# A split-precision MLP up projection: from three matmuls of 256 columns a weight block to one of 512 and one of 256

## The reference

```
x = x + RMSNorm(mixer(RMSNorm(x)))
h = RMSNorm(x)                               # 256 x 2048
h = square(relu(h @ w_up[l])) @ w_down[l]    # w_up 2048 x 8192, w_down 8192 x 2048
x = x + RMSNorm(h)
```

## Time and profile before

| | us |
|---|---|
| median of 3 runs | 2249.34 |
| lowest, highest | 2249.28, 2250.1 |
| span of the profiled execution | 2248.1 |
| PE busy | 2216.5 (99% of the span) |
| DVE busy | 1319.9 (59%) |
| ACT busy | 1016.3 (45%) |

### The profile page before, as it was taken

The page is one execution under the profiler, slowest core; times in us unless marked ns, Lnnn a source line. Parts: engine busy times, 40 slices in busy tenths (PEclk is TensorE's granted clock), DMA queues, the critical chain, the costliest instruction groups (busy, mean ns, idle before and its releaser), DMA issues.

```text
span 2248.1 us, 39497 instructions
## 1 busy us (share of the span) xinstructions
PE 2216.5 (99%) x14282; PEld 2023.7 (90%) x14282; DVE 1319.9 (59%) x1528; ACT 1016.3 (45%) x1280; POOL 109.9 (5%) x112
## 2 busy tenths in 40 slices
PE   8999999999999999999999999999999999999997
PEld 8999888998998998898899988889989989988986
DVE  6777465655555455555578775657554545554555
ACT  5443464543444344344454435545434434443443
POOL 2141000000000000000001410000000000000000
PEclk9999999999999999999999999999999999999999
DMA  6555556556656656655645555655666566556565
GB/s 204 152 170 157 161 188 198 177 179 200 189 180 192 190 179 193 190 184 187 193 125 166 166 161 151 198 185 182 190 192 186 173 201 188 184 189 193 176 194 163
DMA packets 208448, 406.21 MB, mean 181 GB/s; under 512 B 12540, under 2 KB 12820, under 8 KB 207828
## 3 DMA queue, kind: packets, MB, share of 16 engines
q1 hardware_dynamic: 206660, 398.04, 57.3%
q10 hardware_dynamic: 992, 4.78, 0.6%
q0 software_dynamic: 688, 1.90, 0.4%
HBM read 402.58 MB, written 2.10 MB: 180 GB/s over the span
## 4 chain that ended last, share of the span: by engine, by line
issue 71%; PE 26%; DVE 1%; ACT 0%; POOL 0%; DMA 0%; DVEq 0%; POOLq 0%; ACTq 0%
PE acc L734 5%; PE acc L737 5%; PE acc L736 5%; PE acc L699 3%; PE acc L701 3%; PE acc L700 3%; PE M L838 1%; PE M L751 1%; DVE x_sb L1111 0%; PE M L859 0%; DVE xbcT L1177 0%; DMA wk<-in_ssd_out_norm 0%; PE M L879 0%; POOL st L393 0%; DVE w_lo L1028 0%
## 5 line engine op out<-in xcount | busy, mean ns | idle before, releaser
L1028 DVE TENSOR_TENSOR w_lo<-raw,w_hi 128x1024 fp32r<-128x1024 f32 x755 | 927.7, 1235 | 793.4 <-ACT w_hi L462 790.1
L462 ACT ACTIVATE w_hi<-raw 128x1024 fp32r<-128x1024 f32 x755 | 794.5, 1058 | 1026.8 <-PE acc L701 521.6
L734 PE MATMUL acc<-a_hi,w_hi 128*128 128x256 f32 x2912 | 828.4, 284 | 1.8 <-DVE w_lo L1028 1.8
L736 PE MATMUL acc<-a_lo,w_hi 128*128 128x256 f32 x2912 | 823.9, 283 | 0.0
L737 PE MATMUL acc<-a_hi,w_lo 128*128 128x256 f32 x2912 | 823.9, 283 | 0.0
L734 PEld LDWEIGHTS acc<-a_hi,w_hi 128*128 128x128 f32 x2912 | 558.6, 192 | 4.1 <-DVE w_lo L1028 2.7
L736 PEld LDWEIGHTS acc<-a_lo,w_hi 128*128 128x128 f32 x2912 | 558.7, 192 | 1.8 <-issue 1.0
L737 PEld LDWEIGHTS acc<-a_hi,w_lo 128*128 128x128 f32 x2912 | 558.7, 192 | 0.0
L699 PE MATMUL acc<-w_hi,u_hi 128*128 128x512 f32 x1280 | 498.6, 390 | 0.0
L700 PE MATMUL acc<-w_lo,u_hi 128*128 128x512 f32 x1280 | 498.0, 389 | 0.0
L701 PE MATMUL acc<-w_hi,u_lo 128*128 128x512 f32 x1280 | 498.0, 389 | 0.0
(11 more groups left out here) (218 smaller groups left out, 1049.2 us busy)
## 6 DMA issues: line engine op xcount, KB each, us to landing
raw<-in_w_up SPq DMA_DIRECT2D x256, 512.0 KB, 3.7
raw<-in_w_down SPq DMA_DIRECT2D x256, 512.0 KB, 4.5
raw<-in_w_in SPq DMA_DIRECT2D x179, 512.0 KB, 3.8
raw<-in_w_out SPq DMA_DIRECT2D x64, 512.0 KB, 4.6
zg<-in_post_mix_norm ACTq DMA_DIRECT2D x2, 1024.0 KB, 4.6
zg<-in_post_mlp_norm ACTq DMA_DIRECT2D x2, 1024.0 KB, 6.4
out<-x_sb SPq DMA_DIRECT2D x8, 256.0 KB, 2.8
x_sb<-in_x POOLq DMA_DIRECT2D x3, 512.0 KB, 7.3
```

The source lines that it names most:

```text
L462: act.activation(w_hi[:, c % RING], raw[:, c % RING], ACT.Copy).then_inc(sem["hi_ready"], 1)
L734: pe.matmul(o(m), w(w_hi, kk, m), a_hi[:, k], start=(k == 0 and m % 2 == 0), stop=False, skip_group_check=True)
L736: pe.matmul(o(m), w(w_hi, kk, m), a_lo[:, k], start=False, stop=False, skip_group_check=True)
L1028: dve.tensor_tensor(w_lo[:, c % RING], raw[:, c % RING], w_hi[:, c % RING].bitcast(F32), ALU.subtract).then_inc(sem["split_done"], 1)
```

## The change

The parts `a_hi` and `a_lo` become two halves of one tile, `a_both[:, k, 0]` and `a_both[:, k, 1]`. In an up block one matmul of 512 columns streams both through `w_hi`, and one of 256 columns streams `a_hi` through `w_lo`. hi·hi + lo·hi is summed in the left half of a bank and hi·lo in the right half, so a column tile `m` takes a whole bank and a block four. The eight banks are two groups, `wide[0]` (where `acc` lies) and `wide[1]` (where `M` lies), used by `j` = 0 and 1. The down blocks use `acc[1]` and `M[2], M[3]`. After an up block, ACT copies the right halves out, DVE adds the left halves to them, DVE forms relu(x)·x, ACT rounds it into `u_hi`, and DVE subtracts.

```
-        a_hi = sb("a_hi", [P, KT, SEQ], F32R)
-        a_lo = sb("a_lo", [P, KT, SEQ], F32R)
+        a_both = sb("a_both", [P, KT, 2, SEQ], F32R)
...
+        wide = [ctx.enter_context(nc.psum_tensor(f"wide{i}", [P, 4, CB], F32)) for i in range(2)]
+        acc = [[wide[0][:, 2 * i + j] for j in range(2)] for i in range(2)]
+        M = [wide[1][:, i] for i in range(4)]
+        down_acc = [acc[1], [M[2], M[3]]]
+        a_hi, a_lo = a_both[:, :, 0], a_both[:, :, 1]
...
+            def wide_chunk(c, j, lo_ready=None):
...
+                for kk in range(CK):
+                    k = c * CK + kk
+                    for m in range(CB // P):
+                        pe.matmul(wide[j][:, m], w(w_hi, kk, m), a_both[:, k].rearrange("p a s -> p (a s)"),
+                                  start=(k == 0), stop=False, skip_group_check=True)
+                        ins = pe.matmul(wide[j][:, m, 0:SEQ], w(w_lo, kk, m), a_hi[:, k], start=False,
+                                        stop=(k == KT - 1), skip_group_check=True)
+                ins.then_inc(sem["mm_done"], 1)
...
# PE, up_pair
-                        pe.wait_ge(*left(l, B_MLP + j, 0, q * QB + i))
+                        if first:
+                            pe.wait_ge(*left(l, B_OUT + 2, 2))
+                            pe.wait_ge(*left(l, B_OUT + 3, 2))
+                        pe.wait_ge(*up_left(l, j, q * (QB // 2) + i, 0))
+                        pe.wait_ge(*down_left(l, j, q * (QB // 2), 0))
...
-                            feature_chunk(c, 1 - j, upto("xT_ready", l, 8 + 1) if hi_first else None)
+                            wide_chunk(c, j, upto("xT_ready", l, 8 + 1) if hi_first else None)
...
# ACT, up_pair
                         for k in range(2):
+                            act.activation(wk[:, k].rearrange("p (m s) -> p m s", m=2),
+                                           wide[j][:, 2 * k:2 * k + 2, SEQ:2 * SEQ], ACT.Copy)\
+                                .then_inc(sem["right_copied"], 1)
+                        for k in range(2):
                             n = q * (2 * QB) + i * 4 + (2 * j + k)
-                            act.wait_ge(*upto("u_sq", l, n + 1))
-                            act.activation(wk[:, k], acc[1 - j][k][:], ACT.Relu).then_inc(acc_free[1 - j], 1)
-                            act.wait_ge(*left(l, B_MLP + j, k + 1, q * QB + i))
+                            act.wait_ge(*upto("u_sq", l, n + 3))
...
-                            act.activation(u.rearrange("p k s -> p (k s)"), wk[:, k], ACT.Square)\
+                            act.activation(u.rearrange("p k s -> p (k s)"), wk[:, 2 + k], ACT.Copy)\
...
# DVE, up_pair
                         for k in range(2):
+                            dve.wait_ge(*upto("right_copied", l, q * (2 * QB) + i * 4 + (2 * j + k) + 1))
+                            dve.tensor_tensor(wk[:, k].rearrange("p (m s) -> p m s", m=2),
+                                              wide[j][:, 2 * k:2 * k + 2, 0:SEQ],
+                                              wk[:, k].rearrange("p (m s) -> p m s", m=2), ALU.add)\
+                                .then_inc(sem[f"up_left{j}"], 1)
+                        for k in range(2):
+                            dve.wait_ge(*up_left(l, j, q * (QB // 2) + i, k + 1))
+                            dve.scalar_tensor_tensor(wk[:, 2 + k], wk[:, k], 0.0, wk[:, k], ALU.max, ALU.mult)\
+                                .then_inc(sem["u_sq"], 1)
+                        for k in range(2):
                             n = q * (2 * QB) + i * 4 + (2 * j + k)
-                            dve.wait_ge(*left(l, B_MLP + j, k + 1, q * QB + i))
-                            dve.tensor_tensor(wk[:, 2 + k], wk[:, k], wk[:, k], ALU.mult)\
-                                .then_inc(sem["u_sq"], 1)
                             dve.wait_ge(*upto("u_sq", l, n + 3))
```

More of the change, by code:

```diff
@@ L258, in through, with left, up_left, down_left @@
             return sem["mm_done"], RING + chunk(l * NB + b + 1, 0)
-        def left(l, b, n, pairs=0):
-            return acc_free[b % 2], 2 * (l * ((NB + 1 - b % 2) // 2) + b // 2 + pairs) + 2 + n
+        def left(l, b, n):
+            return acc_free[b % 2], 2 * (l * ((B_MLP + 1 - b % 2) // 2) + b // 2) + 2 + n
+        def up_left(l, j, pairs, n):
+            return sem[f"up_left{j}"], l * per["up_left0"] + 2 * pairs + 2 + n
+        def down_left(l, j, pairs, n):
+            return sem[f"down_left{j}"], l * per["down_left0"] + 2 * pairs + 2 + n
         def heads8(a, t, g):
@@ L659, in down_pair @@
                         for t in range(TT):
[L661 removed]
+                            act.wait_ge(*down_left(l, j, q * (QB // 2) + i, t + 1))
                             n = 2 * i + j
@@ L696, in token_chunk @@
                     wh, wl = (w[:, c % RING, kk * CB:(kk + 1) * CB] for w in (w_hi, w_lo))
-                    o = acc[par][t][:]
+                    o = banks[t]
                     sh, sl = (s[:, k, t * P:(t + 1) * P] for s in (s_hi, s_lo))
@@ L738, in feature_chunk, with w @@
                                         skip_group_check=True)
+                ins.then_inc(sem["mm_done"], 1)
+            def wide_chunk(c, j, lo_ready=None):
+                def w(a, kk, m):
+                    return a[:, c % RING, kk * CB + m * P:kk * CB + (m + 1) * P]
+                if lo_ready:
+                    for kk in range(CK):
+                        k = c * CK + kk
+                        for m in range(CB // P):
+                            pe.matmul(wide[j][:, m, 0:SEQ], w(w_hi, kk, m), a_hi[:, k], start=(k == 0), stop=False,
+                                      skip_group_check=True)
+                            pe.matmul(wide[j][:, m, 0:SEQ], w(w_lo, kk, m), a_hi[:, k], start=False, stop=False,
+                                      skip_group_check=True)
+                    pe.wait_ge(*lo_ready)
+                    for kk in range(CK):
+                        for m in range(CB // P):
+                            ins = pe.matmul(wide[j][:, m, SEQ:2 * SEQ], w(w_hi, kk, m), a_lo[:, c * CK + kk],
+                                            start=False, stop=False, skip_group_check=True)
+                    ins.then_inc(sem["mm_done"], 1)
+                    return
+                for kk in range(CK):
+                    k = c * CK + kk
+                    for m in range(CB // P):
+                        pe.matmul(wide[j][:, m], w(w_hi, kk, m), a_both[:, k].rearrange("p a s -> p (a s)"),
+                                  start=(k == 0), stop=False, skip_group_check=True)
+                        ins = pe.matmul(wide[j][:, m, 0:SEQ], w(w_lo, kk, m), a_hi[:, k], start=False,
+                                        stop=(k == KT - 1), skip_group_check=True)
                 ins.then_inc(sem["mm_done"], 1)
@@ L934, in _ @@
                         pe.wait_ge(*left(l, b, 0))
+                    if slot == 0:
+                        pe.wait_ge(*down_left(l, 0, 0, 0))
+                        pe.wait_ge(*down_left(l, 1, 0, 0))
                     take(l * NB + b, c)
@@ L942, in _ @@
                     elif b < B_OUT:
-                        token_chunk(c, b % 2, a_hi, a_lo)
+                        token_chunk(c, acc[b % 2], a_hi, a_lo)
                     else:
-                        token_chunk(c, b % 2, u_hi, u_lo, slot == MIX_SLOTS - 1)
+                        token_chunk(c, acc[b % 2], u_hi, u_lo, slot == MIX_SLOTS - 1)
                     for j in NORM_PE.get(slot, ()):
@@ L995, in down_pair @@
                     for j in range(2):
-                        pe.wait_ge(*left(l, B_MLP + QB + j, 0, q * QB + i))
+                        pe.wait_ge(*up_left(l, j, (q + 1) * (QB // 2), 0))
+                        pe.wait_ge(*down_left(l, j, q * (QB // 2) + i, 0))
                         for c in range(NC):
@@ L1396, in down_pair @@
                                 dve.wait_ge(sem["mm_done"], RING + chunk(b + 1, 0))
-                            dve.tensor_tensor(yp, yp, acc[1 - j][t][:], ALU.add).then_inc(acc_free[1 - j], 1)
+                            dve.tensor_tensor(yp, yp, down_acc[j][t], ALU.add).then_inc(sem[f"down_left{j}"], 1)
                         if last:
```

15 lines of the change are left out of this document (9 added, 6 removed).

## The result

| | before | after |
|---|---|---|
| median us | 2249.38 (4 runs, 2249.28 to 2250.1) | 2235.98 (4 runs, 2235.76 to 2236.23) |
| span of the profiled execution, us | 2248.1 | 2234.3 |
| DVE busy, us | 1319.9 | 1353.3 |
| ACT busy, us | 1016.3 | 1012.9 |

The ratio is 0.9939, 95% interval 0.9925 to 0.9953. The kernel is faster, by 13.4 us; 26.9 us were forecast. The direction was right and the size was twice too large.

The account below looks back on a forecast made before the run. PE's matmul issue in the MLPs was taken as the bound. From the 2248.1 us span, 26.9 us of merged matmuls came off, read-out and waits added 0, and 1.2 us from span to median gave 2222.4 us; range 2220.3 to 2229.0.

Parts of the forecast that it names:

- What bounds the kernel: In both layers' MLPs: PE alone sets the time, in two unbroken "issue" stretches of 701.47 us each.
- The cost line of a matmul: On PE: every matmul with its weight load costs a fixed 13.3 ns plus its columns at 2.4 GHz.
- The count: Up blocks outside each MLP's first chunk: 1016 weight tiles per MLP, two MLPs, 13.24 ns gained each, 26.9 us.
- the forecast's own spread: Uncertainty of the up-block gain: 13.24 ns a tile taken as good to 0.3 ns, some 0.6 us in all.
- the seams: Steps between up and down blocks before the change: 256 to 512 columns 0.12 us, 512 to 256 0.23 us.
- The third rival: Up-block matmuls: most of the fixed part comes back, wide matmul at 237.4 ns, gain 5.4 us, 2243.9 us; chance 3%.
- The read-out behind an up block: ACT and DVE after an up block: chunk 3 split at 6.1 us, needed at 8.0; 44 us more DVE work, cost 0.
- The waits of PE and the refill: PE's new waits for PSUM banks and the later load into chunk 3's slot: both hidden, cost 0.
- The late activations: At up-block ends: serial ACT and DVE chain delays chunk 3's split, PE stalls 32 times, about 2255 us; chance 5%.
- the unmerged matmul: Up blocks: the fixed part does not go, a tile stays at 360 ns, time stays 2249.3 us; chance 3%.
- the fall of the clock: Up blocks: cycling four banks drops the clock to 1.2 GHz, 655 us more, about 2880 us; chance 1%.

Follow-up runs that it names:

- undone merge: Changed kernel's layout and read-out kept, but three matmuls of 256 columns a weight tile as before the change; 2249.37 us against 2249.64 of before.
- turned order: Changed kernel with the narrow matmul (a_hi through w_lo) ahead of the wide one in each weight tile; 2233.17 us.
- 448 and 320: Changed kernel with the two matmuls of a weight tile streaming 448 and 320 columns in place of 512 and 256; 2225.18 us.

## Why the prediction was off

**What bounds the kernel.** Right. PE alone sets the MLP's time, and both long stretches of "issue" stayed unbroken.

**The cost line of a matmul.** Right within a stream of one length: 226.7 ns for 512 columns with four banks in turn, 120.0 for 256, and 173.4 for 384, a length the trace of before did not have. All three have 13.3 ns beside the columns' time at 2.4 GHz. The Trainium skill, TensorE: Matmul & The Clock Gate, section "Back-to-back issue gap", gives 2.5 ns there, for what it calls the isolated gap of a single matmul; the measurement decides.

**The count.** Right: both new lines ran 2032 times outside the first chunks.

**The step that failed** is the sentence "So I price the alternating stream at 226.7 + 120.0", which rested on "Each costs as its first member does in its own stream". The pair costs 353.3 ns, 6.6 more, and that halves a gain of 13.2. I had named the alternating stream as unseen and bounded it by 320 and 360 ns. But then I chose the forecast's own spread, 0.3 ns, as if the seams had settled it. Two things were wrong with the seams. They were read to 0.01 us, while the question was one of 0.013 us. And I looked at one step across each, 0.12 and 0.23 us, which are the steps of the old stream; the effect lies in the six steps behind 496.90. In the alternating stream a step behind a wide matmul takes 236.7 ns where I had 226.7, and one behind a narrow matmul 116.7 where I had 120.0. The third rival, that most of the fixed part comes back, was nearest. Its wide matmul at 237.4 ns was met within 1 ns, but it left the narrow one at 120.0, and the 3.3 ns that the narrow one gives back make half of the gain lost and not four fifths. Its mechanism, the weight load, is not shown. It stood at 3% for 2243.9 us, and the range ended at 2229.0; the measured 2235.98 lies between the two. The 1.2 us carried over from span to median were 1.7 here (2235.98 and 2234.3), which is small beside this.

**The read-out behind an up block.** Right to 0.1 us: chunk 3 split at 6.1 us, ahead of PE's need, which came at 8.3 us where 8.0 was worked out: a chunk takes 2.83 us and not 2.77, and ACT's first copy came 0.2 us behind the block's start and not 0.35. The undone merge shows its price, zero. DVE's busy time rose by 33 us where 44 were worked out: each operation added takes 0.68 us, but the recorded lengths of neighbours overlap. It did not matter.

**The waits of PE and the refill.** Right: no new wait appears in the chain within the MLPs.

**The rivals.** The late activations did not come, nor the unmerged matmul, nor the fall of the clock, which is granted in full. Four banks in turn have no cost with equal or with wide lengths.

**What stays open.** The runs show that changing between 512 and 256 columns costs, how much in each order tried, and that the bank doesn't explain it. They don't show what in PE does it: a cause in the weight loads is not excluded, since their recorded length is the same within 1 ns at either rate (188 ns), and a cause in how the operands are read was not tried apart. Nor do they show why one alternating order settles at 346.7 ns outside the loop and at 353.3 inside (turned order) and another the other way (448 and 320), steadily over whole quarters. That no engine waits, and that the steps of the changed kernel come back every three pairs (236, 233 and 241 ns behind the wide ones, then 236 again), speaks for PE itself, but that is argued and not shown.

## What to carry to other kernels

A cost per matmul that is read from streams of one length does not hold for a stream that mixes lengths: look at the five or six starts behind a seam, and over enough of them for the digits that are asked. Where matmuls of two lengths go to sums that don't mind the order, run each length in long stretches and turn the order from one stretch to the next: here that brought 24.7 us in place of 13.4. Before trusting a gain of some nanoseconds per instruction, give an unseen mixture its whole bound as the range.

## What the runs showed of the hardware

- A growth from 256 to 512 columns costs 27 ns more over the next five matmuls, a fall gives back 7 ns; seen with runs of eight and of sixteen and at the seams between up and down blocks. Where the lengths alternate with every matmul the two together cost 6.6 ns.
- A stream that alternates lengths ran at 346.7 ns a pair in one place and at 353.3 in another of the same kernel (512 and 256 turned; 448 and 320), and kept to either over 70 to 90 us.
- ACT and DVE read two banks in one strided operation (2 x 256 values a partition) in the time of one bank: 595 ns (copy) against 589 (relu) before on ACT, 686 against 684 for an add into `ybuf` on DVE.

```profile
L1425 DVE TENSOR_TENSOR wk<-wide,wk 128x512 f32<-128x512 f32 x64 | 41.2, 686 | 33.4 <-ACT wk L657 33.2
...
L657 ACT ACTIVATE wk<-wide 128x512 f32<-128x512 f32 x64 | 34.8, 595 | 56.5 <-PE wide L786 56.5
```
